# Two dense units behind both heads' level, and VectorE signals that do not wait for VectorE

## The reference, cut to what matters

```python
def step(state, xs):                       # over chunks of the sequence
    b = jnp.cumsum(gb, axis=-2)            # gb: log of the forget gate, per token and key channel
    diff = b[..., :, None, :] - b[..., None, :, :]
    decay = jnp.exp(jnp.where(causal[:, :, None], diff, -jnp.inf))
    scores = jnp.einsum('bhtd,bhsd,bhtsd->bhts', qb, kb, decay)
    o = scores @ ib + jnp.einsum('bhtd,bhdv->bhtv', qb * jnp.exp(b), state)
    ...
y = (o * jax.nn.silu(gh)) ... @ w_out
```

## Time and profile before

| | us |
|---|---|
| median of the three runs | 1653.36 |
| the profiled execution | 1652.83 |
| its span, first to last instruction | 1650.9 |
| PE busy | 1557.8 (94%) |
| DVE busy | 859.8 (52%) |
| ACT busy | 632.2 (38%) |
| POOL busy | 602.8 (37%) |
| the recurrence, first small product to the end of the fourth iteration | about 118 of the 1650.9 |

### The profile page before, as it was taken

One profiled execution on the slowest core, in us unless ns is written; L12 is line 12 of the kernel. 1 busy time (PEld: TensorE's weight loads), 2 busy tenths in 40 slices (PEclk: granted clock), 3 DMA queues, 4 the chain that ended last, 5 costly groups with the idle time before them and its releaser, 6 DMA issues.

```text
span 1650.9 us, 22770 instructions
## 1 busy us (share of the span) xinstructions
PE 1557.8 (94%) x9097; PEld 1206.4 (73%) x9097; DVE 859.8 (52%) x1563; ACT 632.2 (38%) x1140; POOL 602.8 (37%) x452
## 2 busy tenths in 40 slices
PE   7989999999999999998999989989899999999997
PEld 6867666787787666786867766666677877778776
DVE  4882556136863566436249984454485423332224
ACT  6323565354222456444243235745244222122122
POOL 5444211444454211443424342212254444443441
PEclk9999999999999999999999999999999999999999
DMA  9483100234533101233203221101133223323321
GB/s 340 157 293 117 46 27 29 77 137 141 206 100 105 52 29 31 88 128 102 94 26 102 78 82 52 52 26 52 52 117 101 90 78 101 102 77 102 102 77 77
DMA packets 86217, 158.69 MB, mean 96 GB/s; under 512 B 2736, under 2 KB 20704, under 8 KB 86112
## 3 DMA queue, kind: packets, MB, share of 16 engines
q1 hardware_dynamic: 82256, 148.91, 26.9%
q10 hardware_dynamic: 3856, 8.32, 1.4%
HBM read 155.10 MB, written 2.12 MB: 95 GB/s over the span
## 4 chain that ended last, share of the span: by engine, by line
PE 74%; DVE 15%; ACT 3%; issue 3%; DMA 3%; POOL 1%; PEld 1%; SPq 0%; DVEq 0%; ACTq 0%; PEldq 0%
PE banks L395 10%; PE banks L397 10%; PE banks L396 10%; PE banks L391 7%; PE banks L392 7%; PE banks L393 7%; PE banks L491 4%; PE banks L493 3%; PE banks L492 3%; PE banks L516 2%; PE banks L531 2%; PE banks L541 2%; DVE work_lo L1583 2%; POOL w_lo L369 1%; DVE slots L1829 1%
## 5 line engine op out<-in xcount | busy, mean ns | idle before, releaser
L369 POOL TENSOR_TENSOR w_lo<-w_raw,w_hi 128x512 fp32r<-128x512 f32 x440 | 589.3, 1372 | 1011.6 <-ACT w_hi L934 1011.5
L934 ACT ACTIVATE w_hi<-w_raw 128x2048 fp32r<-128x2048 f32 (+1 forms) x112 | 210.8, 1882 | 233.3 <-DMA w_raw<-w_ff_dram 154.2
L391 PE MATMUL banks<-xh,w_hi 128*128 128x512 f32 x640 | 252.5, 395 | 13.2 <-POOL w_lo L369 8.8
L392 PE MATMUL banks<-xl,w_hi 128*128 128x512 f32 x640 | 249.9, 390 | 0.0
L393 PE MATMUL banks<-xh,w_lo 128*128 128x512 f32 x640 | 249.8, 390 | 0.0
L395 PE MATMUL banks<-w_hi,xh 128*128 128x512 f32 x384 | 154.6, 403 | 18.7 <-POOL w_lo L365 9.3
L395 PE MATMUL banks<-w_hi,yh 128*128 128x512 f32 x384 | 152.1, 396 | 8.9 <-issue 4.2
L391 PEld LDWEIGHTS banks<-xh,w_hi 128*128 128x128 f32 x640 | 120.5, 188 | 47.5 <-issue 12.5
L396 PE MATMUL banks<-w_lo,xh 128*128 128x512 f32 x384 | 151.7, 395 | 0.0
L397 PE MATMUL banks<-w_hi,xl 128*128 128x512 f32 x384 | 151.5, 395 | 0.0
L397 PE MATMUL banks<-w_hi,yl 128*128 128x512 f32 x384 | 150.4, 392 | 0.0
(11 more groups left out here) (323 smaller groups left out, 2488.5 us busy)
## 6 DMA issues: line engine op xcount, KB each, us to landing
w_raw<-w_ff_dram SPq DMA_DIRECT2D x32, 1024.0 KB, 5.2
w_raw<-w_in_dram SPq DMA_DIRECT2D x22, 1024.0 KB, 5.1
work_hi<-w_ada_dram SPq DMA_DIRECT2D x16, 1024.0 KB, 7.4
w_raw<-rec_w_in_dram SPq DMA_DIRECT2D x16, 1024.0 KB, 5.4
w_raw<-att_w_in_dram SPq DMA_DIRECT2D x14, 1024.0 KB, 6.8
work_lo<-w_ada_dram SPq DMA_DIRECT2D x8, 1024.0 KB, 8.1
w_raw<-ple_w_gate_dram SPq DMA_DIRECT2D x8, 1024.0 KB, 5.2
w_raw<-att_w_out_dram SPq DMA_DIRECT2D x4, 1024.0 KB, 5.0
```

The source lines that it names most:

```text
L369: ins = pool.tensor_tensor(wlo[s][:, k, :], raw[s][:, k, :], wh[s][:, k, :].bitcast(F32), ALU.subtract)
L391: pe.matmul(out, w_h, x_h, start=start, stop=False)
L392: pe.matmul(out, w_h, x_l, start=False, stop=False)
L934: act.activation(wh[s][:, 0:kn, :], raw[s][:, 0:kn, :], ACT.Copy).then_inc(w_split, 1)
```

## The change

It has two parts. TensorE's units no longer stand one behind each head's small products. Both heads' small products of a level come first, and the units that belong to the level follow, two by two (`REC_UNITS`: one unit at level 4 and one at level 7, two at the others). The number of units in each level, and the two that stand behind L708, stay as they were. And VectorE's decays and conditional copies raise `lev_qk`, `kd_ready` and `lev_kept` themselves, through `then_inc`, without waiting for `dve_self`.

```diff
+REC_UNITS = [(0, 1), (2, 3), (4, 5), (6, 7), (8,), (9, 10), (11, 12), (13,)]
...
                         mm.then_inc(sg("lev_used"), 1)
-                        u = 2 * s + e
-                        for unit in [u] if u < 8 else [] if u == 8 else [u - 1] if u < 15 else []:
-                            beside("g1", 2 * i + unit // 8, unit % 8)
+                    for unit in REC_UNITS[s]:
+                        beside("g1", 2 * i + unit // 8, unit % 8)
...
                     if s == 1:
-                        V.after(dve.tensor_tensor(q_[e], q_[e], feat["B"][:, 2 * i + e, :], ALU.mult))
-                        dve.sem_inc(sg("lev_qk"), 1)
+                        dve.tensor_tensor(q_[e], q_[e], feat["B"][:, 2 * i + e, :], ALU.mult).then_inc(sg("lev_qk"), 1)
                         return
...
-                    V.after(dve.tensor_tensor(x, x, f, ALU.mult))
-                    dve.sem_inc(sg("lev_qk" if s < 8 else "kd_ready"), 1)
+                    dve.tensor_tensor(x, x, f, ALU.mult).then_inc(sg("lev_qk" if s < 8 else "kd_ready"), 1)
...
-                    V.after(dve.copy_predicated(r_near[e].rearrange("p (n c) -> p n c", c=32),
-                                                level[:, s:s + 1, :].broadcast_to([P, TT, 32]),
-                                                ps[:, e, 0:P].rearrange("p (n c) -> p n c", c=32)))
-                    dve.sem_inc(sg("lev_kept"), 1)
+                    dve.copy_predicated(r_near[e].rearrange("p (n c) -> p n c", c=32),
+                                        level[:, s:s + 1, :].broadcast_to([P, TT, 32]),
+                                        ps[:, e, 0:P].rearrange("p (n c) -> p n c", c=32)).then_inc(sg("lev_kept"), 1)
```

## The result

The changed kernel takes 1640.91 us (median of five runs, 1638.79 to 1643.77) against 1653.36 for the kernel before (1650.55 to 1655.71). The ratio is 0.9925, with a 95% interval of 0.9914 to 0.9936: 12.4 us faster. The forecast was 1647.0 with a range down to 1642.5. The profiled span went from 1650.9 to 1639.1 us.

What follows compares the result with a forecast made beforehand. TensorE's stream and VectorE's equal period were taken to pace the recurrence; 5.0 (pairs) + 2.8 (level 7) + 1.4 (level 4) + 0.3 (ScalarE) - 3.2 (GpSimd) = 6.3 us gained, forecast 1647.0 us, range 1642.5 to 1652.5.

Steps and rivals of the forecast that it cites:

- both engines pace the levels: Recurrence levels: TensorE takes 1.29 us a head and VectorE 1.28, so both set the pace at once.
- the parts need each other: Recurrence: pairs with VectorE's old gaps would need 3.16 us on VectorE's path, 0.40 too late for TensorE.
- VectorE's spacings: VectorE without its own waits: decay to copy becomes 0.60 us, copy to decay 0.21.
- the first rival: VectorE's gaps stay at 0.15 us; only 3.2 us gained, 1650; chance 0.12.
- The level after GpSimd's work: Iteration starts beside GpSimd: held decays delay level 2, two levels lose 0.8 us, 2.4 in three iterations.
- The first iteration's levels 0 to 3: GpSimd is busy longer there and covers these levels; they gain nothing, 0.8 us less.
- Level 7's wait: Level 7 to unit 14: unit 13 covers the 0.36 us wait for head 1's decay; 3.30 becomes 2.60, 2.8 us in all.
- the stream in pairs: TensorE at levels 0 to 3, 5 and 6: a level takes 2.37 us instead of 2.58, 5.0 us in all.
- level 4: Head 1's products there wait for the copy; with VectorE 0.48 us quicker a head these waits go, 1.4 us.
- the second rival: Instruction supply: some 14 packet crossings in four iterations each stop TensorE 0.42 us; 4.4 us lost, 1651.5; chance 0.14.
- The third rival: Each of 28 pairs at levels 0 to 6 stops TensorE 0.42 us; 4 us slower, 1657; chance 0.07.
- The fourth: Quicker VectorE slips decays between GpSimd's instructions, half of 3.2 us returns, issue stops shrink; 9 us gained, 1644; chance 0.09.

Runs made afterwards that it cites:

- e1: Changed kernel's units two by two, but VectorE's decays and copies wait for their own end as before; 1651.8 us, ratio 0.9992 to the kernel before.
- e2: Changed kernel's direct VectorE signals, but one unit behind each head as before; 1646.33 us, ratio 0.9962 to the kernel before.
- e3: Changed kernel, but at level 7 unit 13 stands between the heads again; 1645.65 us, ratio 0.996 to the kernel before.
- e6: Changed kernel with the small products of levels 2, 3 and 5 done twice for each head; 1658.18 us, ratio 1.0027 to the kernel before.
- e8: Kernel before, with GpSimd writing zeros in place of the remainder for six chunks of weights; 1646.48 us, ratio 0.9961.
- e4: Changed kernel, but one unit behind each head at level 1, and at level 2 in the first iteration; 1641.37 us, run again 1638.41.
- e7: Changed kernel, with GpSimd writing zeros in place of the remainder for six chunks of weights; 1632.64 us, ratio 0.988 to the kernel before.

## Why the prediction was wrong in size

**What was right.** That both engines pace the levels, and that the parts need each other (e1: nothing; e2: half). VectorE's spacings (0.61 and 0.20 against 0.60 and 0.21): the overlap of the earlier trace rows holds for decays and copies, so the first rival is out. The level after GpSimd's work starting at 6.20 against 6.24. The first iteration's levels 0 to 3 gaining nothing (11.51 to 11.41). Level 7's wait, and that unit 13 is what covers it (e3).

**The step that failed first: the stream in pairs.** The prediction wrote 0.39 + 0.39 for two heads' small products and took "nothing for passing from head 0's small products to head 1's", adding that below nothing it can't go. It can: the 0.39 already held the passage to the unit. A set takes 0.30 (e6), and head 1's passage is paid once a level. Instead of 2.37 a level is 2.28. That is 0.09 at each of 24 such levels, less where decays are held: 0.5 us at levels 0 to 3, 0.7 at levels 5 and 6; and at level 7 2.46 in place of 2.60, 0.6 us in all. Together 1.8 us.

**The second: the kernel before, from which the sum subtracts.** The prediction took every level of the old order as 2 x 1.29, and the lines of the waits table as all that stood beside it. The measured stretches are longer. Levels 2 and 3 took 5.49, 5.39 and 5.83 us in the three later iterations where 5.16 was assumed, and level 4 took 3.39, 2.84 and 2.39 where its work without waits is 2.1. Against the changed kernel that makes some 1.2 us more than forecast at levels 0 to 3 and 1.6 at level 4, the largest miss of a term: 1.4 forecast, 3.0 measured. Most of it, 2.3 us, is the five stops at packets' boundaries in the trace of the kernel before (see e6), such as the 0.42 of the earlier trace rows; the forecast had set those losses at 1.5 and took nothing for them in its sum. Of the rest, some is short waits for copies. The traces of e1, e2 and e8 have none of the five stops. So neither part of the change alone is shown to remove them, and whether other executions of the kernel before have as many is not known; there is one trace of it. With the signals alone, level 4 takes 2.08 to 2.13 us in the later iterations (e2).

With these, 6.3 + 1.8 + 2.8 = 10.9 of the 11.05 measured in the traces. The rest of the 12.4 between medians is the 0.7 us outside the recurrence and the scatter of single executions, about 2 us either way.

**The rivals.** The loss of the second and third rival did not happen: stops without a releaser make about 0.5 us of the changed kernel's recurrence, against 2.3 before. But the second rival named the mechanism that the traces point to. The boundaries are 256 of TensorE's instructions apart, not 312, and two of some 17 stopped it, for about a quarter of a microsecond each, where the rival had 0.42 at every one. e6 shows how near the limit is: twice the small products at three levels brought nearly 9 us of such stops. The third rival tied the stops to pairs of sets; they stand at the packets' boundaries instead. The fourth, decays that slip between GpSimd's instructions, did not happen either; the held decay ends where it did, and the larger gain came from elsewhere. The stops differ between two traces of one kernel (e4: 107.39 and 108.66); why one boundary stops TensorE and another does not is not shown.

## What to carry to other kernels

Sum a change against measured stretches of the old order between fixed points of the program, not against an ideal period plus the listed waits; waits shorter than an instruction, and stops with no name, are in the first and not in the second. For a stop with no name, count the engine's instructions from one to the next and look at the instruction queue's packets. When a group of instructions is priced from start to start, ask what the last gap holds: a passage between kinds of work belongs to the boundary, and disappears with it. Where two engines have equal periods, shorten both in one step, or each part will be priced too low: here nothing and 6 us alone, 12 together.

## What was not expected of the hardware

- VectorE's decay of 128x512 beside GpSimd's subtraction takes up to 1.80 us instead of 0.69, and beside GpSimd's writing of zeros it stays at 0.69 (first iteration of e7). Without the subtraction the changed kernel's recurrence is 9.5 us shorter.
- A signal raised by the instruction itself reaches TensorE 0.15 us after the copy's end (575.34 to 575.49), through the self-wait 0.20 (581.12 to 581.32 in the earlier trace rows).
- TensorE's stops with no releaser stand whole multiples of 256 of its instructions apart, and it goes on 1.22 to 1.53 us after a packet of the instruction queue has landed (22 of 24 stops). They idle it for up to 0.54 us in the kernel before, and for up to 1.54 with 128 small products in a row as recorded (e6).
